# Spreading a gate row over partitions inside an expert turn, not between merge and output projection

## Chip, cores and metric

One NeuronCore of a Trainium2 chip runs the whole kernel. The metric is the device time of one execution in microseconds, and lower is better. Three runs of the kernel before are at hand, and one further execution was taken by the hardware profiler. All times on the span's axis count from its first instruction.

## What is computed

One layer of a hybrid backbone for 384 tokens of width 1024: 128 context tokens and 256 latent tokens, each group with its own conditioning vector. Cut to what matters here:

```
m  = (silu(cond) @ w_ada + b_ada).reshape(6, 1024)      # one m for the context, one for the latent tokens
h  = rmsnorm(x, norm1_g) * (1 + m[1]) + m[0]
x += m[2] * mixer(h)       # attention and a recurrent branch, gated merge, then @ w_out
h  = rmsnorm(x, norm2_g) * (1 + m[4]) + m[3]
x += m[5] * moe(h)         # 64 experts of width 256, 8 for each token, and one shared expert
y  = rmsnorm(x, final_g)
```

The change is about `m[5]`, the gate of the expert part. It is the same for all tokens of a group. It multiplies the shared expert's output and, at the very end, the sum of the routed experts.

## The kernel before

The kernel is written with one instruction list for each engine; the engines meet only through counters (semaphores). An engine works through its list in order, so a wait holds up everything behind it in that list. Nothing but the written order and these waits sets the order of the work.

**Up to the routing.** Tokens are worked on in 3 tiles of 128. The products of the input projection, the merge and the output projection come in three matmuls each (L1052, L1053, L1054): a weight chunk of 128x2048 is split into a high part by ScalarE (`split_high`, L413) and a low part by VectorE (`split_low`, L419). Chunks arrive in 4 raw buffers; the high parts have 2 buffers, so the split of chunk n waits until chunk n - 2 of that list has been used. The merge uses all 8 PSUM banks: banks 0 to 3 for one branch, 4 to 7 for the other, in two passes. VectorE reads each bank once (L1681, L1686, counter `merge_gated`, 16 in all), adds the two (L1689), and ScalarE and VectorE split the sum into `merged_hi` and `merged_lo`. The output projection (`arrived("out", c)`, 4 chunks of 36 products) starts in banks 0 to 2.

**The gate.** The row `m[5]` for both groups is made by the `modulate` matmuls as four partial sums in `m_row[1]`, a tile of 128x1024, to which a DMA adds the bias row (counter `row_biased`, 16 for each row). To be used with tokens on partitions it must stand on all 128 partitions: `spread(1)` on TensorE multiplies it by a matrix of zeros and ones (`pick`), four matmuls of 128x512 into banks 0 and 1 in turn (L1096, counter `bc_mm`), and `spread_copy(1, ...)` on ScalarE copies each result to `gate_ffn` (L834, counter `bc_evac`). `spread(0)` does the same for `m[2]` much earlier, in banks 4 and 5. The first two matmuls of `spread(1)` may start when 12 merge banks have been read; the third and fourth wait for the copies of the first and second. Behind `spread(1)` TensorE transposes the last states of the recurrence (`h_last`, L1266), and then waits for all copies (`bc_evac` 8) before it starts the output projection.

**The experts.** After the output projection come the second norm, the router, the sorting of tokens by expert and the shared expert's gate-up. Then 40 turns follow, in 4 groups of 10 turns and 16 experts. A turn serves one heavy expert (128 rows) or two light ones (64 rows each). The first group is in the order HHHHLLLLLL, the later ones HLLHLHLLHL. A turn's steps on TensorE, in the order of its list: gate-up of turn u into bank 2 or 3 (`gate_up`, L1428), transposes of the next turn's gathered tokens into banks 0 and 1 (`turn_tokens`, L1416), in turns 6 to 8 of the first group (counted from 0) the shared expert's down product (L1339), the down product of the turn before into banks 5 and 6 (`down`, L1447), the transposes of the activations into bank 4 (L1468), and the row numbers of turn u + 3 in bank 7 (L1407). ScalarE's steps are silu (L1022), half of the token copy (L1004), and `y_sb` (L1013); VectorE's are the product with silu (L1910), the other half (L1904), `a_t` from bank 4 (L1914), and the row numbers. GpSimd gathers tokens (L712) and adds results into DRAM (L724) by indirect DMAs.

**The weights' queue.** SP issues all weight loads in one list. The first expert load waits for the last product of the output projection (`out_mm` 12). An expert's gate and up weights (1 MB each, L485) go into one of 5 ring slots as soon as the gate-up of the expert that was there is done (`gu_used`); its down weights (1 MB, L496) after that expert's down product (`dn_used`).

The engine lists around the change, as they stand in the code:

Of the kernel before, what the change touches and what calls it, by code (L numbers as in the profile page):

```python
# [13 lines left out]
P = 128  # L14
D = 1024
KD = D // P
# [46 lines left out]
def hybrid_step(nc, x_prompt, x_sample, cache_k, cache_v, state_f, state_b, c, c_ctx,  # L63
# [5 lines left out]
    with ctx:  # L69
# [32 lines left out]
        pick = little("pick", [P, 2, P])  # L102
# [76 lines left out]
        oa_hi = at("oa_hi", [P, 4, NTOK], EX + 105.125, F32R)  # L179
        ob_hi = at("ob_hi", [P, CT, NTOK], EX + 111.25, F32R)  # L180
        m_row = [at(f"m_row{i}", [P, D], EX + 155.5 + 4 * i) for i in range(2)]
        block_w = at("block_w", [P, 2, 2, CT, P], 12)
# [120 lines left out]
        for n, (kind, i) in enumerate(chunks):  # L303
# [16 lines left out]
            dve_step pool_turn sp_turn num_step onehot_ready idx_mm idx_ready xgt_mm x_first x_second silu_done act_ready  # L320
            at_mm a_ready y_ready x2_ready y_done out_stored""".split()}
        chunk_loaded = [sem(f"chunk_loaded{i}") for i in range(SLOTS + 2)]
# [36 lines left out]

        FIRST_SHARED = 6  # L360


# [185 lines left out]
        def _(pool):  # L548
# [84 lines left out]
            for a in range(4, 6):  # L633
# [3 lines left out]
                pool.dma_start(m_row[a % 2][2:3, :], b_ada[0:1, D * MODS[a]:D * MODS[a] + D]).then_inc(S["row_biased"], 16)  # L637

            pool.wait_ge(S["merge_done"], KD)
            pool.wait_ge(S["merge_mm"], 2 * KD)  # L640
# [109 lines left out]
        def _(act):  # L750
# [79 lines left out]
            def spread_copy(i, dst, scale):  # L830

                for n in range(4):
                    act.wait_ge(S["bc_mm"], 4 * i + n + 1)
                    act.activation(dst[:, n // 2, 512 * (n % 2):512 * (n % 2) + 512], bank[(4, 0)[i] + n % 2][:, :],  # L834
                                   ACT.Copy, scale=scale).then_inc(S["bc_evac"], 1)
# [95 lines left out]
            for m in range(KD):  # L931
# [4 lines left out]
                if m == 3:  # L936
                    split_high(act, number[("pb", 1)])
            spread_copy(1, gate_ffn, 1.0)
            split_high(act, number[("out", 1)])
# [10 lines left out]
            for n in range(number[("out", 2)], number[("out", 3)] + 1):  # L950
                split_high(act, n)
            act.activation(fold_junk[:, :], quarter[:, 0:1], ACT.Sigmoid)
            for t in range(TT):
                act.wait_ge(S["out_done"], TT + t + 1)
                act.activation(xhat2[:, t, :], x_sb[:, t, :], ACT.Square, scale=D ** -0.5,
                               accum_out=sumsq[:, 1, t:t + 1]).then_inc(S["squares_summed"], 1)
# [60 lines left out]
            def block_turn(b, first):  # L1017
                for u in range(UN):
                    i = u if first else b * UN + u
                    experts = turns[first][u]  # L1020
                    act.wait_ge(S["gu_used"], experts[-1] + 1 if first else b * EPG + (experts[-1] + 1))
                    act.activation(silu_sb[:, :], bank[2 + u % 2][:, 0:FE], ACT.Silu).then_inc(S["silu_done"], 1)  # L1022
                    x_copy(i + 1)
                    for t in shared_turn(u, first):
                        shared_out(t)
                    if first and u == 1:
                        act.wait_ge(S["num_step"], 6)
                    if not (first and u == 0):
                        rows_out(i - 1, (u - 1) % UN, experts[0] if first else b * EPG + experts[0])

            x_copy(0)
# [11 lines left out]
        def _(pe):  # L1043
# [45 lines left out]

            def spread(i):  # L1090
                pe.wait_ge(S["pick_made"], 1)
                pe.wait_ge(S["row_biased"], 16 * (i + 1))
                for n in range(4):
                    if 4 * i + n >= 2:
                        pe.wait_ge(S["bc_evac"], 4 * i + n - 1)
                    pe.matmul(bank[(4, 0)[i] + n % 2][:, :], pick[:, n // 2, :], m_row[i][:, 512 * (n % 2):512 * (n % 2) + 512],  # L1096
                              start=True, stop=True).then_inc(S["bc_mm"], 1)

# [87 lines left out]
            modulate(5, 1)  # L1186
            spread(0)
            pe.wait_ge(S["ada_row"], NADA // 2)
# [58 lines left out]
            for i in range(2):  # L1247
                for b, (kind, o) in enumerate((("pa", (oa_hi, oa_lo)), ("pb", (ob_hi, ob_lo)))):
# [3 lines left out]
                    for m in range(4):  # L1252
# [8 lines left out]
                        mm.then_inc(S["merge_mm"], 1)  # L1261
            pe.wait_ge(S["merge_gated"], 2 * KD - 4)
            spread(1)
            pe.wait_ge(S["hl_ready"], 1)
            pe.wait_ge(S["merge_gated"], 2 * KD)
            pe.transpose(bank[6][0:8, 0:P], h_last[:, :], ident[:, :]).then_inc(S["hl_mm"], 1)  # L1266

            pe.wait_ge(S["bc_evac"], 8)
            for c in range(4):
# [181 lines left out]
            def block_turn(b, first):  # L1451
                for u in range(UN):
                    i = u if first else b * UN + u
                    pe.wait_ge(S["x_first"], i + 1)
                    pe.wait_ge(S["x_second"], i + 1)
                    gate_up(u, b, first)
                    turn_tokens(i + 1, u + 1, first)
                    for t in shared_turn(u, first):
# [11 lines left out]
                    pe.wait_ge(S["idx_ready"], 2 * i + 6)  # L1470
                    block_rows(i + 3, u + 3)

            pe.wait_ge(S["num_step"], 6)
# [29 lines left out]
        def _(dve):  # L1503
# [392 lines left out]

            def shared_add(t):
                dve.wait_ge(S["shd_evac"], 2 * t + 2)
                go(dve.tensor_tensor(shared_sb[:, :], shared_sb[:, :], gate_ffn[:, int(t > 0), :], ALU.mult))
# [24 lines left out]
            shared_a(2)  # L1924
            dve.wait_ge(S["bc_evac"], 8)
            block_turn(0, True)
# [52 lines left out]
```

## Time and profile before

| | us |
|---|---|
| median of 3 runs (lowest, highest) | 975.08 (974.1, 976.68) |
| the profiled execution | 981.01 |
| its span, first to last instruction | 979.2 |
| TensorE busy | 870.4 (89% of the span) |
| VectorE busy | 340.4 (35%) |
| ScalarE busy | 248.9 (25%) |
| GpSimd busy | 159.0 (16%) |
| mean granted TensorE clock | 0.955 of full speed |
| moved by DMA | 299.40 MB, mean 306 GB/s |

The profiled execution is one of its own and not among the three runs; what is read from its rows is set against its 981.01 us. Its span is the time on the axis of all rows; 1.8 us lie around it. A busy TensorE is one that has a matmul under way, not one at its peak.

How the rows are to be read: PE is TensorE's matmuls, PEld its weight loads, DVE is VectorE, ACT is ScalarE, POOL is GpSimd, SPq the DMA queue that SP issues to. L-numbers are lines of the kernel before. An fp32 matmul leaves two records, so a count of x16 on L1428 is 8 matmuls, and x4 on L1096 is two; the three-fold products of L1052 to L1054 leave one record each.

### The profile page before, as it was taken

The numbers are of one execution on the slowest core, as the hardware profiler recorded it, in microseconds if no ns is written. First come the engines' busy times: TensorE is split into PE (matmuls) and PEld (weight loads), VectorE is DVE, ScalarE is ACT, GpSimd is POOL, SyncE is SP. The second block draws the span as 40 slices with busy tenths as digits, with TensorE's granted clock in tenths as the row PEclk, the third lists the DMA queues.
The fourth block names the chain that finished last, engine by engine and source line by source line (L and its number), as shares of the span: only waits on it lengthen the run. The fifth ranks groups of instructions, "written<-read, shape, count | busy, mean of one in ns | idle before, by whom it ended". The sixth has DMA issues, their size and how long they took to land.

```text
span 979.2 us, 11593 instructions
## 1 busy us (share of the span) xinstructions
PE 870.4 (89%) x4026; PEld 496.0 (51%) x4026; DVE 340.4 (35%) x833; ACT 248.9 (25%) x415; POOL 159.0 (16%) x221
## 2 busy tenths in 40 slices
PE   4799998999999998999997978979889889888974
PEld 2388775899897754443332433434334334333431
DVE  1653572577564544232421211211112111112115
ACT  2546623444333420112110111111111111111111
POOL 7300000000001330121221212112112212212112
PEclk9799999999999999999997988989999999989988
DMA  9974788222237397799999999999999999999925
GB/s 342 346 274 168 266 292 216 86 88 86 86 129 292 124 365 307 261 336 394 393 397 389 402 389 388 407 387 393 409 391 397 409 393 393 398 392 392 403 55 193
DMA packets 87048, 299.40 MB, mean 306 GB/s; under 512 B 18181, under 2 KB 34625, under 8 KB 62048
## 3 DMA queue, kind: packets, MB, share of 16 engines
q1 hardware_dynamic: 64400, 263.21, 67.8%
q0 software_dynamic: 13904, 31.13, 11.8%
q10 hardware_dynamic: 8704, 4.54, 1.8%
q8 instruction: 24, 0.39, 0.2%
q14 instruction: 16, 0.13, 0.0%
HBM read 287.16 MB, written 29.10 MB: 323 GB/s over the span
## 4 chain that ended last, share of the span: by engine, by line
PE 53%; DMA 32%; SPq 4%; DVE 4%; issue 2%; ACT 2%; POOL 1%; ACTq 1%; POOLq 0%; DVEq 0%
DMA gu<-in_w_up_e_dram 27%; PE bank L1428 16%; PE bank L1052 6%; PE bank L1054 6%; PE bank L1053 6%; PE bank L1447 6%; DMA chunk_raw<-in_w_ada_dram 3%; SPq L485 3%; DMA y_dram<-y_sb,slot_row 2%; PE bank L1321 2%; PE bank L1080 2%; PE bank L1416 1%; PE bank L1121 1%; PE bank L1154 1%; PE bank L1223 1%
## 5 line engine op out<-in xcount | busy, mean ns | idle before, releaser
L1428 PE MATMUL bank<-gu,x_t 128*64 128x512 f32 (+1 forms) x1024 | 308.6, 647 | 57.6 <-DMA gu<-in_w_up_e_dram 56.0
L1428 PEld LDWEIGHTS bank<-gu,x_t 128*64 128x64 f32 (+1 forms) x1024 | 110.1, 162 | 224.2 <-issue 197.7
L1447 PE MATMUL bank<-dn,a_t 128*64 128x512 f32 (+1 forms) x512 | 145.3, 597 | 4.8 <-ACT shared_sb L987 3.5
L724 POOL DMA_INDIRECT y_dram<-y_sb,slot_row x39 | 62.6, 1606 | 444.0 <-issue 253.5
L1910 DVE TENSOR_TENSOR act_sb<-silu_sb,bank 128x256 f32<-128x256 f32 x40 | 16.8, 421 | 306.0 <-ACT silu_sb L1022 306.0
L1022 ACT ACTIVATE silu_sb<-bank 128x256 f32<-128x256 f32 x40 | 15.3, 384 | 326.5 <-PE bank L1428 326.5
L1447 PEld LDWEIGHTS bank<-dn,a_t 128*64 128x64 f32 (+1 forms) x512 | 48.5, 150 | 74.8 <-issue 67.4
L1052 PE MATMUL bank<-h_hi,chunk_lo 128*128 128x384 f32 x240 | 85.1, 355 | 0.0
L1013 ACT ACTIVATE y_sb<-bank,slot_gate 128x512 f32<-128x512 f32 x80 | 50.6, 683 | 126.1 <-PE bank L1447 97.6
L1053 PE MATMUL bank<-h_lo,chunk_hi 128*128 128x384 f32 x240 | 81.3, 339 | 0.0
L1054 PE MATMUL bank<-h_hi,chunk_hi 128*128 128x384 f32 x240 | 81.3, 339 | 0.0
L1914 DVE COPY a_t<-bank 128x256 f32<-128x256 f32 x40 | 17.0, 424 | 138.2 <-PE bank L1468 138.2
L419 DVE TENSOR_TENSOR chunk_lo<-chunk_raw,chunk_hi 128x2048 fp32r<-128x2048 f32 x25 | 57.1, 2286 | 19.4 <-ACT chunk_hi L413 19.3
L413 ACT ACTIVATE chunk_hi<-chunk_raw 128x2048 fp32r<-128x2048 f32 x25 | 47.7, 1913 | 50.4 <-PE bank L1054 50.3
L712 POOL DMA_INDIRECT xg<-h_dram,slot_tok x42 | 45.7, 1087 | 50.2 <-DVE slot_row L1800 22.6
L1416 PEld LDWEIGHTS bank<-ident,xg 128*128 128x128 f32 x328 | 36.4, 141 | 27.9 <-issue 27.9
L1052 PEld LDWEIGHTS bank<-h_hi,chunk_lo 128*128 128x128 f32 x240 | 45.7, 190 | 7.2 <-issue 5.6
L1053 PEld LDWEIGHTS bank<-h_lo,chunk_hi 128*128 128x128 f32 x240 | 45.8, 191 | 0.3
L1054 PEld LDWEIGHTS bank<-h_hi,chunk_hi 128*128 128x128 f32 x240 | 45.8, 191 | 0.0
L1416 PE MATMUL bank<-ident,xg 128*128 128x128 f32 x328 | 43.9, 277 | 0.0
L1004 ACT ACTIVATE x_t<-bank 128x512 f32<-128x512 f32 x41 | 24.5, 597 | 23.4 <-PE bank L1416 23.4
L1904 DVE COPY x_t<-bank 128x512 f32<-128x512 f32 x41 | 28.3, 691 | 4.2 <-PE bank L1416 2.6
(335 smaller groups left out, 940.8 us busy)
## 6 DMA issues: line engine op xcount, KB each, us to landing
gu<-in_w_gate_e_dram SPq DMA_DIRECT2D x64, 1024.0 KB, 19.1
gu<-in_w_up_e_dram SPq DMA_DIRECT2D x64, 1024.0 KB, 25.2
dn<-in_w_down_e_dram SPq DMA_DIRECT2D x64, 1024.0 KB, 25.5
chunk_raw<-in_w_ada_dram SPq DMA_DIRECT2D x24, 1024.0 KB, 8.9
chunk_raw<-in_w_in_dram SPq DMA_DIRECT2D x18, 1024.0 KB, 5.3
chunk_raw<-in_w_out_dram SPq DMA_DIRECT2D x4, 1024.0 KB, 5.0
y_dram<-zeros POOLq DMA_DIRECT2D x1, 3072.0 KB, 18.0
chunk_raw<-in_w_pa_dram SPq DMA_DIRECT2D x2, 1024.0 KB, 5.0
```

What stands on the lines that cost most here:

```text
L413: act.activation(chunk_hi[j % HIGHS][:, :], chunk_raw[slot[n]][:, :], ACT.Copy).then_inc(S["chunk_high"], 1)
L419: dve.tensor_tensor(chunk_lo[slot[n]][:, :], chunk_raw[slot[n]][:, :], chunk_hi[j % HIGHS][:, :].bitcast(F32), ALU.subtract).then_inc(S["c ...
L485: sp.dma_start(gu[k][:, 2048 * g:2048 * g + 2048], w[0, e].rearrange("a (p k) n -> (a p) (k n)", k=KD)).then_inc(gu_ready[k], 16)
L712: pool.indirect_dma_start(xg[u % 2][:, :], None, h2_dram[:, :], bass.IndirectOffsetOnAxis(ap=slot_tok[:, u % UN:u % UN + 1], axis=0), boun ...
L724: pool.indirect_dma_start(y_dram[:, :], bass.IndirectOffsetOnAxis(ap=slot_row[:, u % UN:u % UN + 1], axis=0), y_sb[u % 2][:, :], None, bou ...
L1013: ins = act.activation(y_sb[u % 2][:, half * 512:half * 512 + 512], bank[5 + half][:, :], ACT.Copy, scale=slot_gate[:, u:u + 1])
L1052: pe.matmul(out, left[1], right[0], start=start, stop=False)
L1053: pe.matmul(out, left[0], right[1], start=False, stop=False)
L1054: return pe.matmul(out, left[0], right[0], start=False, stop=stop)
L1416: mm = pe.transpose(bank[k // 4][:, (k % 4) * P:(k % 4 + 1) * P], xg[u % 2][:, k * P:(k + 1) * P], ident[:, :])
L1428: mm = pe.matmul(bank[2 + u % 2][at_x, :].rearrange("p (g n) -> p g n", g=2), x_t[:, cols], wide[:, :, k, :], start=(k == 0), stop=(k == K ...
L1447: mm = pe.matmul(bank[5 + half][at_x, :], a_t[:, cols], dn[slot_of(x, first)][:, wc], start=(k == 0), stop=(k == 1))
```

## The change

It takes `spread(1)` and its copies out of the place between merge and output projection and puts them at the end of the first group's fifth turn (u = 4 counted from 0).

- TensorE: no spread, and no wait for `bc_evac` 8, ahead of the output projection. In the fifth turn, behind the row numbers, it waits for the next turn's tokens (`x_first`, `x_second`) and for `a_t` (`a_ready`), and does the four matmuls without a wait between them, into banks 3, 0, 1 and 4. The sixth turn's gate-up waits until bank 3 has been copied (`bc_evac` 5), the transposes behind it until all four have (`bc_evac` 8).
- ScalarE: the four copies stand behind `y_sb` of the fifth turn; the third waits for all four matmuls. The split of chunk 1 of the output projection is now right behind the last `merged_hi`.
- GpSimd: by then the tile `m_row[1]` is overwritten by the second norm's `xhat2`. So GpSimd copies it to `m_late` (128x1024, counter `late_row`) once the last input projection is done. `m_late` lies in the second half of `gate_ffn`; this is why the third copy waits for the last matmul. ScalarE waits for `late_row` before it writes `xhat2`.
- VectorE: its wait for the copies moves from ahead of the first turn into the shared expert's addition.

No matmul or copy of the spread is dropped; one copy on GpSimd is added.

```
@@
+            pool.wait_ge(S["w_mm"], NPROJ)
+            pool.wait_ge(S["row_biased"], 32)
+            pool.tensor_copy(m_late[:, :], m_row[1][:, :]).then_inc(S["late_row"], 1)
             pool.wait_ge(S["merge_done"], KD)
@@ ScalarE
-                    act.wait_ge(S["bc_mm"], 4 * i + n + 1)
-                    act.activation(dst[:, n // 2, 512 * (n % 2):512 * (n % 2) + 512], bank[(4, 0)[i] + n % 2][:, :],
+                    act.wait_ge(S["bc_mm"], 8 if i and n == 2 else 4 * i + n + 1)
+                    act.activation(dst[:, n // 2, 512 * (n % 2):512 * (n % 2) + 512], (spread_bank(n) if i else bank[4 + n % 2])[:, :],
@@
-            spread_copy(1, gate_ffn, 1.0)
             split_high(act, number[("out", 1)])
@@
             act.activation(fold_junk[:, :], quarter[:, 0:1], ACT.Sigmoid)
+            act.wait_ge(S["late_row"], 1)
@@ behind rows_out of a turn
+                    if first and u == SPREAD_TURN:
+                        spread_copy(1, gate_ffn, 1.0)
@@ TensorE, between merge and output projection
-            pe.wait_ge(S["merge_gated"], 2 * KD - 4)
-            spread(1)
             pe.wait_ge(S["hl_ready"], 1)
             pe.wait_ge(S["merge_gated"], 2 * KD)
             pe.transpose(bank[6][0:8, 0:P], h_last[:, :], ident[:, :]).then_inc(S["hl_mm"], 1)
 
-            pe.wait_ge(S["bc_evac"], 8)
@@ TensorE, in a turn
+                    if first and u == SPREAD_TURN + 1:
+                        pe.wait_ge(S["bc_evac"], 5)
                     gate_up(u, b, first)
+                    if first and u == SPREAD_TURN + 1:
+                        pe.wait_ge(S["bc_evac"], 8)
                     turn_tokens(i + 1, u + 1, first)
@@
                     block_rows(i + 3, u + 3)
+                    if first and u == SPREAD_TURN:
+                        pe.wait_ge(S["late_row"], 1)
+                        pe.wait_ge(S["x_first"], i + 2)
+                        pe.wait_ge(S["x_second"], i + 2)
+                        pe.wait_ge(S["a_ready"], i + 1)
+                        for n in range(4):
+                            spread(n, spread_bank(n), m_late)
@@ VectorE
             def shared_add(t):
+                dve.wait_ge(S["bc_evac"], 8)
                 dve.wait_ge(S["shd_evac"], 2 * t + 2)
@@
             shared_a(2)
-            dve.wait_ge(S["bc_evac"], 8)
             block_turn(0, True)
```

TensorE's list between the merge (the last row on `ob_hi`) and the output projection (the first on `merged_lo`), before:

```order
L1054 MATMUL bank7<-ob_hi_135,chunk_hi0_99 128x384
L1096 MATMUL bank0<-m_row1_137,pick_55 128x512 [waits row_biased,bc_evac,pick_made,merge_gated]
L1096 MATMUL bank1<-m_row1_137,pick_55 128x512 [waits bc_evac]
L1096 MATMUL bank0<-m_row1_137,pick_55 128x512 [waits bc_evac]
L1096 MATMUL bank1<-m_row1_137,pick_55 128x512 [waits bc_evac]
L1266 MATMUL bank6<-ident_52,h_last_77 8x128 [waits merge_gated,hl_ready]
L1052 MATMUL bank0<-chunk_hi1_100,merged_lo_104 128x512 [waits merged_ready,chunk_ready,bc_evac]
```

The same place after the change (the lines of the code have moved by 11 and 9):

```order
L1065 MATMUL bank7<-ob_hi_135,chunk_hi0_99 128x384
L1275 MATMUL bank6<-ident_52,h_last_77 8x128 [waits merge_gated,hl_ready]
L1063 MATMUL bank0<-chunk_hi1_100,merged_lo_104 128x512 [waits merged_ready,chunk_ready]
L1064 MATMUL bank0<-chunk_lo0_95,merged_hi_105 128x512
L1065 MATMUL bank0<-chunk_hi1_100,merged_hi_105 128x512
```

The four matmuls are gone, and with them the projection's wait for ScalarE's copies.

TensorE's list at the end of the first group's fifth turn, after the change (L1455 down, L1480 activations, L1415 row numbers, L1102 the spread, L1436 the sixth turn's gate-up):

```order
L1455 MATMUL bank6<-dn3_157,a_t_167 128x512 x2
L1480 MATMUL bank4<-ident_52,act_sb_145 128x128 [waits act_ready]
L1480 MATMUL bank4<-ident_52,act_sb_145 128x128
L1415 MATMUL bank7<-row_tab_169,onehot1_171 128x8 [waits onehot_ready,idx_ready]
L1415 MATMUL bank7<-row_tab_169,onehot1_171 128x8 x2
L1102 MATMUL bank3<-m_late_136,pick_55 128x512 [waits x_second,a_ready,x_first,late_row]
L1102 MATMUL bank0<-m_late_136,pick_55 128x512
L1102 MATMUL bank1<-m_late_136,pick_55 128x512
L1102 MATMUL bank4<-m_late_136,pick_55 128x512
L1436 MATMUL bank3<-gu1_150,x_t_162 64x512 [waits gu_ready1,bc_evac,gu_ready2,x_second,x_first]
```

The four matmuls stand ahead of the sixth turn's gate-up, with the wait for `a_ready` ahead of them.

## Rows read from the trace of the kernel before

**Rows 1.** The page, 40 equal slices of the span: the DMA engines' busy share.

```profile
DMA  9974788222237397799999999999999999999925
```

**Rows 2.** Stretches: span, busy times, then granted clock, DMA share, GB/s.

```profile
426.00:434.00 8.00, 8.00 (x37) 3.46 (x34) 2.27 (x8) 0.98 (x2) 2.00 (x2) 1.00 0.82 228
434.00:470.00 36.00, 34.82 (x166) 13.21 (x166) 12.32 (x41) 6.84 (x12) 8.81 (x6) 1.00 1.02 394
470.00:920.00 450.00, 395.14 (x1624) 165.87 (x1621) 85.17 (x285) 71.77 (x128) 81.27 (x61) 0.94 1.02 396
```

**Rows 3.** Timeline, 295 to 302 us: start, duration, what, [idle before, releaser].

```profile
295.36 0.34 PE L1054 MATMUL bank<-ob_hi,chunk_hi 128*128 128x384 f32 x1
295.53 1.88 PE L1096 MATMUL bank<-m_row,pick 128*128 128x512 f32 x4
296.12 0.55 DVE L1686 SCALAR_TENSOR_TENSOR gb<-gb,bank 128x384 f32<-128x384 f32 x1
298.36 1.98 PE L1096 MATMUL bank<-m_row,pick 128*128 128x512 f32 x4 [0.94 <-ACT gate_ffn L834]
300.18 0.27 PE L1266 MATMUL bank<-ident,h_last 128*8 128x128 f32 x1
301.03 0.50 PE L1052 MATMUL bank<-chunk_hi,merged_lo 128*128 128x512 f32 x1 [0.58 <-ACT gate_ffn L834]
```

**Rows 4.** The chain of waits, 295 to 302 us: start, duration, what.

```profile
297.29 0.52 ACT merged_hi L935
...
300.38 0.61 ACT gate_ffn L834
300.98 0.04 issue
```

**Rows 5.** Timeline: chunk 1 of the output projection, and the first expert load.

```profile
300.87 1.91 ACT L413 ACTIVATE chunk_hi<-chunk_raw 128x2048 fp32r<-128x2048 f32 x1
302.81 2.29 DVE L419 TENSOR_TENSOR chunk_lo<-chunk_raw,chunk_hi 128x2048 fp32r<-128x2048 f32 x1 [4.40 <-ACT chunk_hi L413]
334.00 0.33 SPq L485 DMA_DIRECT2D gu<-in_w_gate_e_dram  x1
```

**Rows 6.** Timeline: a GpSimd copy, the last input projection, VectorE behind it.

```profile
19.88 1.05 POOL L605 COPY rpb_rep<-rpb_pad 56x1024 f32<-56x1024 f32 x1
259.25 0.34 PE L1054 MATMUL bank<-h_hi,chunk_hi 128*128 128x384 f32 x1
262.73 0.56 DVE L1664 TENSOR_TENSOR oa_lo<-oa_t,oa_hi 128x384 fp32r<-128x384 f32 x1 [4.40 <-ACT oa_hi L917]
```

**Rows 7.** Timeline: gate-ups of the first group's fifth and sixth turn, and between them.

```profile
423.31 7.09 PE L1428 MATMUL bank<-gu,x_t 128*64 128x512 f32 x32
434.90 1.26 ACT L1013 ACTIVATE y_sb<-bank,slot_gate 128x512 f32<-128x512 f32 x2 [2.84 <-PE bank L1447]
435.07 7.09 PE L1428 MATMUL bank<-gu,x_t 128*64 128x512 f32 x32
435.12 0.42 DVE L1914 COPY a_t<-bank 128x256 f32<-128x256 f32 x1 [2.97 <-PE bank L1468]
442.32 0.33 SPq L485 DMA_DIRECT2D gu<-in_w_gate_e_dram  x1
```

**Rows 8.** DMA issues at 434.37 and at 448.88 us: us to landing.

```profile
gu<-in_w_up_e_dram SPq DMA_DIRECT2D x1, 1024.0 KB, 19.5
gu<-in_w_up_e_dram SPq DMA_DIRECT2D x1, 1024.0 KB, 24.0
```

**Rows 9.** Timeline: gate-ups of the tenth and the twelfth turn.

```profile
498.40 7.09 PE L1428 MATMUL bank<-gu,x_t 128*64 128x512 f32 x32 [0.73 <-DMA gu<-in_w_up_e_dram]
529.40 9.95 PE L1428 MATMUL bank<-gu,x_t 128*64 128x512 f32 x32 [6.89 <-DMA gu<-in_w_up_e_dram]
```

**Rows 10.** Stretches, with the columns of Rows 2: granted clock behind two pauses.

```profile
458.80:459.90 1.10, 0.00 (x0) 0.00 (x0) 0.00 (x0) 1.06 (x2) 0.00 (x0) 1.00 1.01 413
529.00:535.00 6.00, 5.60 (x14) 1.92 (x16) 0.00 (x0) 0.00 (x0) 0.00 (x0) 0.50 1.03 352
```

More of the change, by code:

```diff
@@ L180, in hybrid_step @@
         ob_hi = at("ob_hi", [P, CT, NTOK], EX + 111.25, F32R)
+        m_late = at("m_late", [P, D], 28)
         m_row = [at(f"m_row{i}", [P, D], EX + 155.5 + 4 * i) for i in range(2)]
@@ L320, in hybrid_step @@
             dve_step pool_turn sp_turn num_step onehot_ready idx_mm idx_ready xgt_mm x_first x_second silu_done act_ready
-            at_mm a_ready y_ready x2_ready y_done out_stored""".split()}
+            at_mm a_ready y_ready x2_ready y_done out_stored late_row""".split()}
         chunk_loaded = [sem(f"chunk_loaded{i}") for i in range(SLOTS + 2)]
@@ L360, in hybrid_step, with spread_bank @@
         FIRST_SHARED = 6
+        SPREAD_TURN = 4
+        def spread_bank(n):
+            return bank[(2 + (SPREAD_TURN + 1) % 2, 0, 1, 4)[n]]
         first_half = (("router_loaded", 16), ("shared_loaded", 48), ("bias_loaded", 32))
@@ L1088, in turn_rows, with spread @@
                 mm.then_inc(S["m_spread"], 1)
[L1090 to L1097, printed above, removed]
+            def spread(n, out, row):
+                pe.matmul(out[:, :], pick[:, n // 2, :], row[:, 512 * (n % 2):512 * (n % 2) + 512],
+                          start=True, stop=True).then_inc(S["bc_mm"], 1)
             for a in range(2):
@@ L1186, in _ @@
             modulate(5, 1)
-            spread(0)
+            pe.wait_ge(S["pick_made"], 1)
+            pe.wait_ge(S["row_biased"], 16)
+            for n in range(4):
+                if n >= 2:
+                    pe.wait_ge(S["bc_evac"], n - 1)
+                spread(n, bank[4 + n % 2], m_row[0])
             pe.wait_ge(S["ada_row"], NADA // 2)
@@ L1471, in block_turn @@
                     block_rows(i + 3, u + 3)
+                    if first and u == SPREAD_TURN:
[3 more added lines that the diff above has]
+                        pe.wait_ge(S["a_ready"], i + 1)
+                        for n in range(4):
+                            spread(n, spread_bank(n), m_late)
             pe.wait_ge(S["num_step"], 6)
```

## The prediction

> **What bounds the kernel.** I read the page first, its 40 slices of 24.5 us: the digits of the DMA share are 2 and 3 in slices 8 to 12 and 9 from slice 18 (416 us) to 38 [rows 1]. So the kernel has two parts with different limits: up to the routing a chain through TensorE, ScalarE and VectorE, then a part paced by the stream of expert weights. The view of stretches draws the border: the DMA share is 0.82 from 426 to 434 us and 1.02 from 434 to 920 us [rows 2]. A delay of TensorE costs its full length before 434 us; behind it, only what outlasts the stock of transfers.
>
> Next the place that the change clears, in order of time [rows 3]. The last product of the merge starts at 295.36 us, and VectorE has read its bank at 296.12 + 0.55 = 296.67 us. The spread of the gate runs from 295.53 to 300.34 us. An fp32 matmul leaves two records, so "x4" is two matmuls: two in 1.88 us, then 0.94 us of waiting until ScalarE has emptied a bank, then two in 1.98 us. The transpose of the last states follows (300.18 us, 0.27 us), and the first product of the output projection at 301.03 us, after 0.58 us for ScalarE's fourth copy. The chain of waits [rows 4] runs through the same pieces: ScalarE's merged_hi at 297.29, the spread's second half, ScalarE's copy at 300.38 us. The spread lies on the path.
>
> **What goes.** After the change TensorE needs two things before the output projection: the 16 gated merge banks (296.67 us, unchanged) and the transpose. From a signal to the engine I count 0.04 us, the "issue" piece in [rows 4]. The first product then starts at 296.67 + 0.04 + 0.27 = 296.98 us, 4.05 us before 301.03. Bounds: 4.3 us if the transpose hides behind the wait; 3.5 us if the product follows the signal as late as it followed the transpose's start in [rows 3], by 301.03 - 300.18 = 0.85 us, a wait for ScalarE included. I take 4.0 us.
>
> Does another wait take the place? The projection starts with chunk 0; its 144 products take 334.00 - 301.03 = 33.0 us, 0.229 us each [rows 3, 5], so chunk 1 is needed 36 products later, at 305.2 us in the new time. Its high half stood behind the four copies on ScalarE (300.87 us, 1.91 us), its low half behind that on VectorE (302.81 us, 2.29 us) [rows 5]. ScalarE is now free at 297.29 + 0.52 = 297.81 us, so the low half is ready at 297.81 + 1.91 + 2.29 = 302.0 us: 3 us to spare. Chunks 2 and 3 wait for products and move along. The first expert load leaves the SP queue at 334.00 us, on the last product's signal [rows 5]; it, the router and the sorting hang on that product. What does not move is GpSimd's zero fill of y_dram, issued at the merge's end; the DMA share falls from 7 in slice 13 to 3 in slice 14 (318 to 343 us) [rows 1], so it has drained before that load. Zero.
>
> **What is added on GpSimd.** One copy of 128x1024, once the last input projection is done (259.25 us) [rows 6]. The nearest row is the copy of 56x1024, 1.05 us. The engine has nothing else to do there. It could slow VectorE through SBUF, but VectorE idles for 4.40 us until 262.73 us [rows 6], and 259.6 + 1.05 = 260.7 lies inside. Zero; if they met, at most 1.05 us on oa_lo, which TensorE waits for. ScalarE's late_row (before the second squares) and VectorE's bc_evac 8 (now only before the shared expert's addition, two turns on) are met long before. Zero each.
>
> **What is added in the first group's fifth turn.** Its gate-up starts at 423.31 us, the sixth turn's at 435.07 us [rows 7], without idle time between. TensorE now waits behind the row sums for a_t: that copy ends at 435.12 + 0.42 = 435.54 us, 0.5 us after the sixth gate-up used to start. Then come four matmuls of 128x512, all in a row: twice the 1.88 us of [rows 3] is 3.75, a little less without the edges; 3.6 us. They end at 435.58 + 3.6 = 439.2 us. ScalarE is done with y_sb at 434.90 + 1.26 = 436.16 us and empties bank 3 (full at 436.5) by 437.1 us, so the wait at the head of the sixth gate-up is met; the copies of banks 1 and 4 follow the fourth matmul and end by 440.4 us, before the transposes that stand 7 us behind the gate-up's start. The slip is 0.5 + 3.6 = 4.1 us (bounds 3.5, with a_t's wait hidden, and 4.9, with one exposed copy of 0.6 us and signals). It is as long as the gain, so all depends on who pays for it.
>
> Who waits for TensorE there? The next load leaves the SP queue at 442.32 us, after the sixth gate-up [rows 7]; with the slip, 4.1 us later against the stream. But the load issued at 434.37 us lands 19.5 us later, at 453.9 us [rows 8]: the DMA engines have 11.6 us of work in stock when the load at 442.32 is issued, and would still have 7.5. The load issued at 448.88 us takes 24.0 us, so the stock grows. The slip is taken from it. TensorE does not wait for weights from the sixth to the ninth turn; at the tenth it already waits 0.73 us for a load (498.40 us) and two turns on 6.89 us (529.40 us) [rows 9]. A TensorE that is late against the stream by 4.1 us comes 4.1 - 0.7 = 3.4 us behind the tenth's load and waits 3.4 us less at the twelfth. I cost the slip at nothing: its covers are the stock of 11.6 us, then the wait of 6.89 us. Without them it costs 4.1 us.
>
> **The sum.** The profiled execution's 981.01 us (span 979.2 and 1.8 around it) less 4.0 is 977.0 us. The median shown, 975.08 us, is 0.6% below this execution; the same step gives **971.1 us**.
>
> **The rivals.** *Exposed slip.* The sixth turn comes late and the end with it: 975.08 - 4.0 + 4.1 = 975.2 us, no difference; half exposed, 973.1. For it: TensorE has no pause between the fifth and sixth turn, and the slip is long. Against it: the stock and the 6.89 us.
>
> *The clock (slower).* TensorE now pauses in one piece from 295.70 (295.36 + 0.34) to 296.7 us, where matmuls of the spread ran, and for 0.5 us in the fifth turn. If the granted clock falls to its lower level there, the matmuls behind take twice as long. What that costs: after the pause of 6.89 us the clock is 0.50 (1.2 GHz) from 529 to 535 us, and the gate-up takes 9.95 us against 7.09: 2.86 us more [rows 7, 9, 10]. With both pauses hit and the sixth turn uncovered the sum is 975.08 - 4.0 + 2.86 + 4.1 + 2.86 = 980.9 us. It decides once its losses pass 4.0 us, some 18 products of 0.229 us at the lower level. Against it: over the pause from 458.8 to 459.9 us, in which TensorE does nothing, the clock stays at 1.00 (2.4 GHz) [rows 10], and neither new pause is longer.
> The Trainium skill (TensorE: Matmul & The Clock Gate, "A second HAM failure mode: psum-queue depth-cycling") says that a kernel which cycles through PSUM banks can pause briefly so often between groups of matmuls that its clock swings between the levels. By that rule this rival would be likely; the trace disagrees, with 1.00 over the pause of 1.1 us.
>
> *No effect ahead.* Another wait takes the place of the one removed, or the weight stream does not start earlier: 975.1 us. Against it: the 3 us to spare for chunk 1, and the release of the first load. What I could have missed is a wait of the routing stage on something that does not move.
>
> **The chances.** Forecast 0.69; slip exposed in whole or half 0.18; no effect ahead 0.07; the clock 0.06. A measurement of this kernel can tell about 0.3% (2.9 us) from no change. The forecast lies 1.1 us above that bound, and its own bounds and the spread of the runs (974.1 to 976.68) take a few hundredths across; the exposed slip and no effect lie within. So faster 0.66, same 0.27, slower 0.07. The range goes from 969.6 us (4.3 gained, and 1.2 of spread between medians) to 975.3 us, over the exposed slip; it leaves out the clock and the tails.
>
> **What would show it.** The last merge product at 295.4 us as before, the first of the output projection near 297.0, the first expert load near 330.0. The fifth turn's gate-up near 419.3, then eight records from m_late, the sixth near 435.2 (15.9 us after the fifth, not 11.8); the DMA share at 1.0 from about 430 us all the same; the tenth near 497.8, with no wait; the twelfth near 525.4, after some 3.5 us of waiting; the end 4 us earlier. I am wrong on the first term if the first product starts after 297.5; on the cover if the DMA share between 432 and 470 us shows a hole, or the twelfth gate-up starts after 527 us; on the slip if the sixth follows the fifth by other than 15.2 to 16.7 us.

## The result, and the profile after

The changed kernel takes 969.6 us (median of 9 runs, 966.62 to 972.54), the kernel before, run beside it, 975.98 us (9 runs, 973.18 to 980.95). The ratio is 0.9938, with a 95% interval from 0.9921 to 0.9956: the change saves 6.0 us, between 4.3 and 7.7. The forecast was 971.1 us and a saving of 4.0; the measured median lies on the lower edge of its range (969.6 to 975.3). The profiled execution of the changed kernel took 972.46 us (span 970.7, mean granted clock 0.960), against 981.01 us before (979.2, 0.955).

The place that was cleared, in the order of time on TensorE after the change (start, duration, engine, line, operation, count, idle time before it and who ended it; L1065 is the last of the three products, L1275 the transpose of `h_last`). It answers to [rows 3].

```profile
294.63 0.34 PE L1065 MATMUL bank<-ob_hi,chunk_hi 128*128 128x384 f32 x1
296.09 0.27 PE L1275 MATMUL bank<-ident,h_last 128*8 128x128 f32 x1 [1.12 <-DVE gb L1705]
296.21 0.47 PE L1063 MATMUL bank<-chunk_hi,merged_lo 128*128 128x512 f32 x1
```

From the last merge product to the first product of the projection it is 296.21 - 294.63 = 1.58 us. Before it was 301.03 - 295.36 = 5.67 us [rows 3]. The difference is 4.09 us. On the axis of the span the first product comes 4.82 us earlier, but 0.73 us of that is a merge that ended earlier in this execution, which the change does not touch. The end of the merge moves from execution to execution: between 290.89 us (c3, below, whose code is the same up to there) and 295.36 us (before) in these profiles.

TensorE and ScalarE at the end of the fifth turn, in the order of time (L1102 is the spread, L843 its copies, L1436 the gate-up, L1455 the down product); it answers to [rows 7].

```profile
418.46 7.09 PE L1436 MATMUL bank<-gu,x_t 128*64 128x512 f32 x32
425.48 1.09 PE L1424 MATMUL bank<-ident,xg 128*128 128x128 f32 x8
426.41 3.60 PE L1455 MATMUL bank<-dn,a_t 128*128 128x512 f32 x8
429.84 0.39 PE L1480 MATMUL bank<-ident,act_sb 128*128 128x128 f32 x2
430.07 0.22 PE L1415 MATMUL bank<-row_tab,onehot 128*128 128x8 bf16 x3
430.84 3.67 PE L1102 MATMUL bank<-m_late,pick 128*128 128x512 f32 x8 [0.55 <-DVE a_t L1934]
434.44 7.09 PE L1436 MATMUL bank<-gu,x_t 128*64 128x512 f32 x32
...
430.05 1.26 ACT L1022 ACTIVATE y_sb<-bank,slot_gate 128x512 f32<-128x512 f32 x2 [2.84 <-PE bank L1455]
431.98 0.60 ACT L843 ACTIVATE gate_ffn<-bank 128x512 f32<-128x512 f32 x1 [0.67 <-PE bank L1102]
432.83 0.60 ACT L843 ACTIVATE gate_ffn<-bank 128x512 f32<-128x512 f32 x1 [0.26 <-PE bank L1102]
434.55 1.09 ACT L843 ACTIVATE gate_ffn<-bank 128x512 f32<-128x512 f32 x2 [1.12 <-PE bank L1102]
```

The sixth gate-up follows the fifth by 434.44 - 418.46 = 15.98 us, where it was 435.07 - 423.31 = 11.76 us [rows 7]. So the slip is 4.22 us: 0.55 us of waiting for `a_t`, the four matmuls in a row, no wait for a bank. In absolute time the sixth turn starts where it did (434.44 against 435.07). The turns behind it start at the old time too, until a weight load decides. The stretches around the slip (columns of the stretches: busy time and count on PE, PEld, DVE, ACT, POOL; granted clock; DMA share; GB/s), beside [rows 2]:

```profile
426.00:434.00 8.00, 7.45 (x27) 3.72 (x25) 4.50 (x18) 3.06 (x6) 1.57 (x1) 1.00 0.89 313
434.00:470.00 36.00, 34.82 (x164) 12.79 (x162) 9.02 (x26) 6.67 (x12) 7.25 (x5) 1.00 1.02 403
```

The twelfth turn's gate-up, beside [rows 9], and the page's line of the DMA share in 40 slices, beside [rows 1]:

```profile
524.09 8.47 PE L1436 MATMUL bank<-gu,x_t 128*64 128x512 f32 x32 [3.01 <-DMA gu<-in_w_up_e_dram]
```
```profile
DMA  9975779322247497799999999999999999999925
```

There is no hole in the stream of weights behind the slip: the DMA share is 1.02, as before, and 9 in all slices from 18 to 38. The twelfth gate-up starts 5.3 us earlier than before, after a wait of 3.01 us instead of 6.89 us.

One profile is one execution, and the one of the kernel before is long in a part that the change hardly touches. The first expert load, here in the change and in a2 (below, the kernel before with added work in the fifth turn), divides the span:

```profile
329.16 0.33 SPq L491 DMA_DIRECT2D gu<-in_w_gate_e_dram  x1
332.80 0.33 SPq L485 DMA_DIRECT2D gu<-in_w_gate_e_dram  x1
```

| profile | last merge product to first load | first load to the end of the span |
|---|---|---|
| before | 38.64 us | 645.2 us |
| a2, slip alone | 38.64 us | 641.2 us |
| c3, before, pauses filled | 38.69 us | 640.6 us |
| the change | 34.53 us | 641.5 us |
| a1, the change again | 34.53 us | 641.6 us |
| a3, gain alone | 34.53 us | 640.4 us |

So the first part is 4.11 us shorter in every profile with the early projection, and the rest is as long as it is in a2 and c3. The 645.2 us are those of one execution: times of the twelfth turn that are compared with it hold up to 4 us that are not the change's.

### The profile page after: what moved, and what is told of

It reads as the page before. It is cut to its first block, busy times and chain, and to the rows that moved or that the text cites. A ratio compares the mean times of both kernels' runs of the same rounds, so it can differ in the third digit from the quotient of the medians.

```text
span 970.7 us, 11597 instructions
## 1 busy us (share of the span) xinstructions
PE 866.5 (89%) x4026; PEld 493.5 (51%) x4026; DVE 340.7 (35%) x833; ACT 249.3 (26%) x415; POOL 162.3 (17%) x222
## 4 chain that ended last, share of the span: by engine, by line
PE 55%; DMA 31%; SPq 4%; DVE 4%; issue 2%; ACT 2%; POOL 1%; ACTq 1%; POOLq 0%; DVEq 0%
DMA gu<-in_w_up_e_dram 26%; PE bank L1436 17%; PE bank L1063 6%; PE bank L1065 6%; PE bank L1064 6%; PE bank L1455 6%; DMA chunk_raw<-in_w_ada_dram 3%; SPq L491 3%; PE bank L1091 2%; PE bank L1329 2%; PE bank L1424 2%; PE bank L1127 1%; DMA y_dram<-y_sb,slot_row 1%; PE bank L1160 1%; PE bank L1102 1%
## 5 line engine op out<-in xcount | busy, mean ns | idle before, releaser
L1436 PE MATMUL bank<-gu,x_t 128*64 128x512 f32 (+1 forms) x1024 | 305.5, 640 | 52.8 <-DMA gu<-in_w_up_e_dram 51.1
L1436 PEld LDWEIGHTS bank<-gu,x_t 128*64 128x64 f32 (+1 forms) x1024 | 109.0, 160 | 218.1 <-issue 193.1
L1455 PE MATMUL bank<-dn,a_t 128*64 128x512 f32 (+1 forms) x512 | 145.3, 597 | 4.8 <-ACT shared_sb L996 3.5
L1455 PEld LDWEIGHTS bank<-dn,a_t 128*64 128x64 f32 (+1 forms) x512 | 48.5, 150 | 74.8 <-issue 67.4
L1065 PE MATMUL bank<-h_hi,chunk_hi 128*128 128x384 f32 x240 | 81.1, 338 | 0.0
L1065 PEld LDWEIGHTS bank<-h_hi,chunk_hi 128*128 128x128 f32 x240 | 45.3, 189 | 0.0
```

The lines of the kernel that those rows point to most:

```text
L1065: return pe.matmul(out, left[0], right[0], start=False, stop=stop)
L1436: mm = pe.matmul(bank[2 + u % 2][at_x, :].rearrange("p (g n) -> p g n", g=2), x_t[:, cols], wide[:, :, k, :], start=(k == 0), stop=(k == K ...
L1455: mm = pe.matmul(bank[5 + half][at_x, :], a_t[:, cols], dn[slot_of(x, first)][:, wc], start=(k == 0), stop=(k == 1))
```

## The experiments

One theory and its rivals stood at the start. The **stock theory** is the prediction's: what TensorE does earlier up to the routing counts in full, and the slip in the fifth turn is paid by transfers in stock and by the twelfth turn's wait. The rivals: the slip costs something and the gain ahead is larger than 4 us; or the gain comes from elsewhere (the clock, the place itself, or, as rival L, a stream that runs faster when TensorE is late against it). Kernels of one group (a, b, c) ran on one chip and share the runs of the kernel before.

### The change again

The changed kernel without an edit, as the measure beside a2 to a4.

> The changed kernel itself, beside the others on one chip. Theory S (the stock of transfers pays the 4.2 us slip, nothing else changes): ratio 0.9958, 4.1 us less. Rival L (a TensorE that is late against the stream makes the stream itself run a little faster, which would be the 2 us beyond the forecast): 0.9938 again, 6 us less.

Measured: 970.05 us (6 runs) against 975.55, ratio 0.9929 (0.9902 to 0.9957). The gain is there a second time, and again nearer 6 than 4 us, though the interval reaches from 4.2 to 9.6 us. The ratio is the one that rival L expected; a3 decides on it.

### The slip alone

The kernel before, with four matmuls in the fifth turn behind the same waits; their results are not used.

```
+                    if first and u == 4:
+                        pe.wait_ge(S["x_first"], i + 2)
+                        pe.wait_ge(S["x_second"], i + 2)
+                        pe.wait_ge(S["a_ready"], i + 1)
+                        for n in range(4):
+                            pe.matmul(bank[(3, 0, 1, 4)[n]][:, :], pick[:, n // 2, :], ...)
```

> The kernel before, with four more matmuls of 128x512 at the end of the first group's fifth turn, with the waits of the change and with results that nobody reads; the spread stays between merge and output projection. Theory S: the sixth gate-up comes 15.9 us after the fifth and the end does not move, ratio 1.000. Rival L: 2 us less, 0.998. Rival E (the slip is exposed): 4.2 us more, 1.0043.

Measured: 975.83 us (12 runs), ratio 0.9993 (0.9974 to 1.0012). The slip of some 4 us is in the trace (the sixth gate-up 15.98 us behind the fifth, 436.39 against 420.41 us) and no cost of it is seen. The interval reaches from 2.5 us gained to 1.2 us lost: it excludes the exposed slip of 4.2 us, not rival L's gain of 2 us.

### The gain alone

The changed kernel without its spread, its copies and the waits for them in the fifth and sixth turn; the gate is a constant.

```
-            pool.tensor_copy(m_late[:, :], m_row[1][:, :]).then_inc(S["late_row"], 1)
+            pool.memset(gate_ffn[:, :, :], 1.0).then_inc(S["late_row"], 1)
...
-                    if first and u == SPREAD_TURN:
...
-                        for n in range(4):
-                            spread(n, spread_bank(n), m_late)
```

> The changed kernel without the spread and its copies: GpSimd fills the expert part's gate with the constant 1.0, so this part of the computation is left out, and the fifth turn has no added matmuls. Theory S: the first product of the output projection as early as in the change, no slip, ratio 0.9958 (4.1 us less), the same as the change. Rival L: also 0.9958, but 2 us more than the change. Rival E: 4.2 us less than the change.

Measured: 969.86 us (7 runs), ratio 0.9935 (0.9911 to 0.9958). Taking the fifth turn's work away altogether brings nothing that can be seen beyond the change (970.05; the difference is 0.2 us, with some 1.5 us to either side). Rival L expected 2 us more time than the change; that lies outside. The twelfth gate-up of this kernel shows where the 4 us go that it does not spend in the fifth turn:

```profile
520.89 8.73 PE L1434 MATMUL bank<-gu,x_t 128*64 128x512 f32 x32 [7.19 <-DMA gu<-in_w_up_e_dram]
```

It waits 7.19 us; the change waits 3.01, and 2.47 in a1, where this gate-up starts at 521.05 us, 0.2 us from this one. The slip is exchanged for a wait that is there anyway.

### The spread in the second turn

```
-        SPREAD_TURN = 4
+        SPREAD_TURN = 1
```

> The changed kernel with the spread in the first group's second turn, where TensorE paces the transfers and the DMA engines have holes. Theory S: a slip of 4.2 us there moves all later loads, the stream begins its closed stretch no earlier than in the kernel before, so gain and slip cancel: ratio 1.000 (0.999 to 1.001). Rival G (the stream would catch up anyway, wherever the slip is): 0.9958 or less, as in the change.

Measured: 974.9 us (12 runs), ratio 0.9987 (0.9970 to 1.0003). The projection starts as early as in the change (295.46 us), but the same 4 us, spent before the stream of weights is full, come out behind it: the twelfth gate-up at 525.11 us against 521.05 in a1. The gain is lost, the interval leaves at most 2.9 us of it. The distance by itself is not enough; where the moved work is put decides.

### The slip doubled, and fourfold

The changed kernel with four further matmuls of 128x512 ahead of the spread; in the fourfold kernel the added loop runs over `range(12)`.

```
+                        for n in range(4):
+                            pe.matmul(spread_bank(n % 4)[:, :], pick[:, 0, :], m_late[:, 0:512], start=True, stop=True)
                         for n in range(4):
                             spread(n, spread_bank(n), m_late)
```

> The changed kernel with four more matmuls of 128x512, whose results are overwritten, ahead of the spread in the fifth turn: a slip of 7.8 instead of 4.2 us. Theory S: the stock at the next load is 11.6 us in the kernel before, and the twelfth turn waited 6.89 us, so nearly all of it is still covered: at most 1 us more than the change, ratio 0.994 to 0.995. Rival E (cover is thin): 3.6 us more than the change, 0.9975.

> The changed kernel with twelve more matmuls of 128x512, a slip of 15 us in the fifth turn. Theory S: more than the stock of 11.6 us at the next load, so the DMA share shows a hole between 430 and 460 us, and TensorE is late by more than the twelfth turn's wait; 3 to 9 us more than the change, ratio 0.997 to 1.003. Rival C (the stream catches up with any slip): no more than the change, 0.994.

Measured: doubled 971.21 us, ratio 0.9977 (0.9952 to 1.0002); fourfold 978.27 us, ratio 1.0042 (1.0017 to 1.0067); 12 runs each. The expectation for the doubled slip, at most 1 us more than the change, was missed, and the fourfold's 1.0042 lies just above its upper end, 1.003. The fifth and sixth gate-ups, doubled:

```profile
416.57 7.09 PE L1436 MATMUL bank<-gu,x_t 128*64 128x512 f32 x32
...
436.00 7.09 PE L1436 MATMUL bank<-gu,x_t 128*64 128x512 f32 x32
```

its stretch behind them:

```profile
434.00:470.00 36.00, 34.83 (x159) 12.93 (x159) 8.64 (x23) 7.39 (x14) 5.53 (x4) 1.00 0.96 373
```

and fourfold, the gate-ups:

```profile
415.07 7.09 PE L1436 MATMUL bank<-gu,x_t 128*64 128x512 f32 x32
...
441.36 7.09 PE L1436 MATMUL bank<-gu,x_t 128*64 128x512 f32 x32
```

and the stretches, the second one with the deepest part of the hole:

```profile
434.00:470.00 36.00, 34.82 (x144) 13.34 (x143) 4.00 (x12) 6.67 (x13) 2.63 (x2) 1.00 0.78 297
440.00:450.00 10.00, 10.00 (x48) 3.74 (x48) 0.91 (x2) 2.31 (x5) 0.00 (x0) 1.00 0.21 63
```

This gives the stock its size. The slips are 436.00 - 416.57 - 11.76 = 7.67 us and 441.36 - 415.07 - 11.76 = 14.53 us. The DMA share over these 36 us falls from 1.02 to 0.96 and to 0.78, which is 36 x 0.06 / 1.02 = 2.1 us and 36 x 0.24 / 1.02 = 8.5 us of missing transfers. What the stock paid is then 7.67 - 2.1 = 5.6 us and 14.53 - 8.5 = 6.0 us: some 6 us, not the 11.6 us of the prediction.

The holes account for the times. The nearest measure is b4 (the spread in the sixth turn, below), from the same chip and free of a hole. The doubled slip takes 2.0 us more than b4, the fourfold 9.0 us more, each with 2 to 3 us to either side; the holes are 2.1 and 8.5 us. The profiles say the same more sharply: from the first load to the end of the span it is 640.4 us in a3, 641.6 in a1, 641.9 doubled and 648.7 fourfold. By these runs a slip is free up to about 6 us and costs what goes beyond, and the change's 4.22 us lies 1.5 us inside; the doubled slip's cost alone is at the edge of what the runs can tell.

The fourfold slip also shows why the reading of the stock was too large. These are its last load ahead of the hole, the first behind it, and the stretch in which the transfers ran out:

```profile
426.12 0.45 SPq L491 DMA_DIRECT2D gu<-in_w_up_e_dram  x1
448.61 0.33 SPq L491 DMA_DIRECT2D gu<-in_w_gate_e_dram  x1
441.00:442.00 1.00, 1.00 (x5) 0.34 (x6) 0.00 (x0) 0.53 (x2) 0.00 (x0) 1.00 0.31 131
```

With nothing issued behind it, the DMA engines ran dry some 15 us after the load at 426.12 us. The like load of the kernel before took 19.5 us to land [rows 8], with further loads issued from 442.32 us on, 8 us behind it. That those took a share of the engines from it is argued, not shown; the 15 us are.

### The spread in the sixth turn

```
-        SPREAD_TURN = 4
+        SPREAD_TURN = 5
```

> The changed kernel with the spread in the first group's sixth turn, one turn later, where the stock is larger. Theory S: the same as the change, ratio 0.994 (0.992 to 0.996 by its two measurements). Rival P (the fifth turn is special): another time by over 1.5 us.

Measured: 969.24 us (12 runs), ratio 0.9954 (0.9930 to 0.9978). As good as the fifth turn, not better in a way that can be told.

### Four banks at the old place

The kernel before, with its spread in banks 0 to 3 and no wait between the four matmuls; the projection waits tile by tile for the copies.

```
-                    act.activation(dst[...], bank[(4, 0)[i] + n % 2][:, :],
+                    act.activation(dst[...], bank[n if i else 4 + n % 2][:, :],
...
-            spread(1)
+            for n in range(4):
+                pe.matmul(bank[n][:, :], pick[:, n // 2, :], m_row[1][...], start=True, stop=True)
...
-            pe.wait_ge(S["bc_evac"], 8)
...
+                    if c == 0:
+                        pe.wait_ge(S["bc_evac"], 5 + t)
```

> The spread stays between merge and output projection, but goes into banks 0 to 3 at once, with no wait for ScalarE between its matmuls, and the projection's three tiles wait for their own bank only. Theory S (every microsecond before the stream counts once): the two pauses of 0.94 and 0.58 us go, the four matmuls of 3.7 us stay; the first product starts near 299.5 on the scale on which it started at 301.03: 1.5 us less, ratio 0.9985. Rival M (removing anything there is worth more than its length, since the change gained 6 us for 4.1 us): 0.9975 or less.

Measured: 978.12 us (12 runs: two at 971.4 and 971.8, ten from 977.6 to 979.9), ratio 1.0034 (1.0010 to 1.0058). Slower than the kernel before, where both expectations had it faster, though its profile shows the projection 2.0 us nearer to the merge (3.64 us behind its last product, where it was 5.67). The loss is behind the projection, at the second norm and the router. TensorE there, in the order of time:

```profile
329.83 0.40 PE L1054 MATMUL bank<-chunk_hi,merged_hi 128*128 128x512 f32 x1
330.07 1.04 PE L1299 MATMUL bank<-ident,xhat 128*128 128x128 f32 x8
332.40 1.16 PE L1299 MATMUL bank<-ident,xhat 128*128 128x128 f32 x8 [1.29 <-DVE xhat L1514]
334.68 1.67 PE L1299 MATMUL bank<-ident,xhat 128*128 128x128 f32 x8 [1.12 <-DVE xhat L1514]
336.15 10.34 PE L1306 MATMUL bank<-w_router_sb,h_t 128*128 128x64 f32 x48
```

and the same place in a1, the changed kernel:

```profile
330.51 1.16 PE L1300 MATMUL bank<-ident,xhat 128*128 128x128 f32 x8 [1.29 <-DVE xhat L1526]
332.79 1.16 PE L1300 MATMUL bank<-ident,xhat 128*128 128x128 f32 x8 [1.12 <-DVE xhat L1526]
333.79 5.47 PE L1307 MATMUL bank<-w_router_sb,h_t 128*128 128x64 f32 x48
```

The pauses are the same to the hundredth, 1.29 and 1.12 us; the router's matmuls take 10.34 us against 5.47. The stretches of the four banks kernel (columns as above) show why:

```profile
330.00:334.00 4.00, 2.27 (x17) 1.84 (x16) 3.47 (x8) 2.42 (x8) 1.76 (x6) 1.00 0.66 238
334.00:336.00 2.00, 1.32 (x8) 1.32 (x9) 2.00 (x6) 1.65 (x5) 2.00 (x19) 0.79 0.97 406
336.00:341.00 5.00, 5.00 (x26) 5.00 (x24) 1.17 (x4) 1.50 (x4) 4.74 (x12) 0.50 1.03 436
341.00:347.00 6.00, 6.00 (x30) 6.00 (x30) 0.01 (x1) 0.33 (x1) 3.71 (x5) 0.50 1.00 419
```

At the second pause the granted clock falls to 0.50 (1.2 GHz) and stays there for over 12 us. In c1, the same kernel again, it is at 0.50 in the whole stretch from 334 to 336 us, so there it fell inside the pause, which ends at 334.59 us. From the last product of the projection to the first gate-up it is 51.0 us in this kernel and 44.9 in the change (328.28 to 373.20 us).

### The same, with the pauses filled

Four kernels: the four banks once more as the control (c1); the four banks (c2), the kernel before (c3) and the spread in the sixth turn (c4), each with further transposes in the two pauses, whose results are not used:

```
             for t in range(TT):
                 turn_rows2(t)
+                if t < TT - 1:
+                    pe.wait_ge(S["out_done"], TT)
+                    for j in range(8):
+                        pe.transpose(bank[2][...], xhat2[:, t, j:D:KD], ident[:, :])
```

> The four banks version of b1, once more, as the control beside the next one. Theory C (the pause clock): the timing with which TensorE enters the second norm decides whether its granted clock falls in the router stage. Then most runs lie 6 to 7 us above the few others, the median is again near 978 (ratio about 1.003), and the profile, if it is of the long kind, shows the router's 48 matmuls at about 10.1 us and a granted clock of 0.50 there. Rival D (b1's loss was something of that session or place, not of the kernel): median near 973, ratio about 0.998, router 5.3 us.

> The four banks version, and in TensorE's two pauses of the second norm (1.29 and 1.12 us) eight further transposes each of the rows that are there already, into bank 2, which nobody reads; they add nothing to what is computed. Theory C: the pauses are what lets the clock fall, so with them filled the router's 48 matmuls take 5.3 us, the stretch from the last projection matmul to the first gate-up 45 us and not 51, the median is near 972.5 (ratio 0.998, the 2 us by which the projection starts earlier) and runs of the long kind are gone. If only the length of the stage or the order of banks sets it, nothing changes against the control: near 978, router 10.1 us.

> The kernel before with the same two fillings. If the kernel before, too, falls now and then into the low clock in the router stage, the fillings take its long runs away: its median falls by 1 to 2 us against the kernel before (ratio 0.998 to 0.999) and its spread narrows from some 7 us. That would be the part of the change's gain beyond the 4.1 us of the distance from merge to projection. If it never does, the ratio is 1.000, within 0.1%, and the rest of the gain is not of this place.

> The change with its spread in the sixth turn (b4) and the two fillings. The change's profiles show no low clock in the router stage, so theory C expects the same as b4, ratio 0.995 (about 970), with at most the long runs gone; as a version to keep it would be worth no more than 1 us. If the fillings cost (they hold up the next transposes by what they run over the pause, at most 0.1 us each) nothing of it is visible.

| kernel | median (runs) | ratio to before (interval) | router's matmuls in the profile |
|---|---|---|---|
| c1, four banks | 977.28 (12) | 1.0014 (0.9991 to 1.0038) | 10.3 us |
| c2, four banks, filled | 971.71 (12) | 0.9965 (0.9944 to 0.9986) | 5.5 us |
| c3, before, filled | 972.95 (12) | 0.9993 (0.9977 to 1.0008) | 5.5 us |
| c4, sixth turn, filled | 969.25 (6) | 0.9944 (0.9925 to 0.9962) | 5.5 us |

TensorE in c2, in the order of time, with L1315 the added transposes:

```profile
331.27 1.06 PE L1315 MATMUL bank<-ident,xhat 128*128 128x128 f32 x8
332.73 1.16 PE L1299 MATMUL bank<-ident,xhat 128*128 128x128 f32 x8 [0.40 <-DVE xhat L1518]
333.72 1.04 PE L1315 MATMUL bank<-ident,xhat 128*128 128x128 f32 x8
335.01 1.16 PE L1299 MATMUL bank<-ident,xhat 128*128 128x128 f32 x8 [0.25 <-DVE xhat L1518]
336.00 5.47 PE L1306 MATMUL bank<-w_router_sb,h_t 128*128 128x64 f32 x48
```

and the stretch of its router:

```profile
336.00:341.00 5.00, 5.00 (x48) 5.00 (x46) 1.50 (x5) 1.51 (x4) 4.74 (x17) 1.00 1.00 421
```

With the pauses filled, work that nobody needs makes the four banks kernel 5.6 us faster by the medians (some 1 to 8 us), and 11 of its 12 runs lie below 974 us (the twelfth at 977.68), where 18 of the 24 of b1 and c1 lay above 975. So the low clock in the router stage is what slowed it. The added work hardly shifts the stage: from the first to the third set of the needed transposes it is 335.01 - 330.39 = 4.62 us, against 334.68 - 330.07 = 4.61 in b1. What it takes away is TensorE's idle time (0.40 and 0.25 us are left of 1.29 and 1.12), so that has a part in the fall; what else has is not shown. c3 is unclear: the interval holds both no effect and 2 us, the medians (972.95 against 974.94) differ by the 2 us, and its profile shows what the kernel before showed, 5.5 us. c4 is as good as b4 and the change; none of the three can be told from the others, and no run here beats the change beyond doubt.

## Why the prediction was right, and where it was off

- **What goes: right.** Forecast 4.05 us between merge and projection, measured 4.09. Chunk 1 had room, as said: its low half was ready at 301.2 us. The transpose now stands 1.12 us behind the last merge product.
- **GpSimd's copy: right.** It took 1.04 us from 258.93 us, and VectorE's idle time ahead of oa_lo is 4.40 us as in [rows 6].
- **The slip: right, term by term.** 0.55 us of waiting for `a_t` against 0.5, the matmuls 3.67 us against 3.6; 4.22 us against 4.1 in all, the sixth gate-up 15.98 us behind the fifth against 15.9.
- **Who pays: right in kind, wrong in size.** The slip alone shows no cost (a2), leaving it out brings nothing (a3), and ahead of the full stream it costs its full length (a4). The step "the DMA engines have 11.6 us of work in stock" failed in its size: b2 and b3 measure some 6 us. I had read the stock from the time a load took to land, 19.5 us [rows 8]; with nothing issued behind it, the transfers ran out some 15 us after such a load's issue (b3). The margin was 1.5 us, not 7.5. The rival of the exposed slip was nearer than its argument against it said.
- **The twelfth turn: right in kind, its numbers in part by luck.** Forecast a wait of 3.5 us and a start at 525.4; measured 3.01 us and 524.09, 0.7 us of it the earlier merge. The same program started this gate-up at 521.05 us in a1, and a2, with no early projection, at 525.79 us after 2.77 us of waiting, so one profile cannot confirm a start to 1 us.
- **No effect ahead: refuted** by a1 and a3. What sets the end is the first load, and with it the projection: 34.53 us behind the merge instead of 38.64, and some 641 us to the end either way (a2, c3, the change, a1).
- **The clock: no loss in the change, but a real danger next door.** I had looked at the two pauses that the change makes, and both leave the clock at 1.00. b1 shows the fall at pauses which every version has and no other profile suffers from, 35 us behind the edit. My argument against it (a pause of 1.1 us leaves the clock at 1.00 [rows 10]) holds for that pause and not for another of 1.12 us. The Trainium skill (TensorE: Matmul & The Clock Gate, "A second HAM failure mode: psum-queue depth-cycling") says of a bf16 kernel that cycles through PSUM banks that brief idling between its groups of matmuls swings the clock between its levels. Here, with fp32 transposes and other pauses, the traces of b1 and c1 (0.50) agree that brief pauses can do it, and that of a1 does not, with the same two pauses at 1.00.
- **The size of the gain: about 1.5 us more than the sum, and the time just inside the range.** The measured 969.6 us is the range's lower edge, so the time was met with some luck. The versions with the early projection and no slip beyond the stock gained 6.0, 6.9, 6.3, 4.5 and 5.4 us by their ratios (the change, a1, a3, b4, c4), each with an interval of 1.7 to 2.7 us to either side. All lie above 4.09, but a1 and a3 share one set of runs of the kernel before, and one set stood for b4, b2 and b3: with their holes added these two come to 4.3 and 4.4 us, as b4 did. It is not the slip, since a3 has none and shows it too. The profiles show 4.11 us up to the first load, and behind it only the kernel before's own profile is longer (645.2 us against 641.2 in a2). Whether the kernel before runs into such long executions more often than the change was not measured; c3 was to test one cause of them, the clock at the router, and stays unclear. This part stays open.

## What to carry to other kernels

When a step leaves the path and must be done elsewhere, look for a place where the engine's lateness is already being waited for, and measure the depth of that cover by putting 2 and 4 times the work there; here a slip of 4 us was free and one of 8 us no longer. The time a transfer takes to land overstated the stock by a factor of two here; a hole in the DMA share of the stretch behind is the sign to look for. Where one profile of each kernel is compared, split the span at a landmark that both have, since here the part ahead of the edit moved by 4 us between executions of the same code. And before you credit or blame an edit, compare the granted clock of the stretches far behind it: an edit that brought TensorE 2 us forward came with a loss of 6 us elsewhere.

## What the hardware showed that was not expected

The granted clock is not set by the length of the last pause. With pauses of 1.29 and 1.12 us around the same eight transposes, the router's 48 matmuls ran at 1.00 (5.47 us) in the profiles of the change and at 0.50 (10.34 us) with four banks. From the output projection to the router TensorE's list is the same but for the projection's waits for the copies; ahead of it the two differ in the spread. The same four banks program seems to do both: of its 24 runs six lie from 970.7 to 973.4 us and eighteen above 975 (both of its profiles are of the second kind), and 16 unneeded transposes brought the median to 971.7. The kernel before and the changed one were at 1.00 there in every profile. What in the timing ahead of the pauses decides was not tried.
